# Sample attention of a streaming encoder step: appended new keys, hi/lo latent scores, one stacked rotary product, key scales spread by DMA

## The chip, the cores and the metric

The kernel runs on one core of a Trainium2 chip. The metric is the device time of one execution in microseconds (us), the median of three runs. Five engines work side by side, each with its own list of instructions, and wait for one another only through semaphores: TensorE (PE, matrix products; its weight loads are listed as PEld), VectorE (DVE), ScalarE (ACT), GpSimd (POOL) and SyncE (SP). PE reads SBUF and writes PSUM, which has eight banks of 512 fp32 columns. Every engine works through its own list strictly in the order in which it is written, so a wait at one place holds back all that stands behind it on that engine.

## The reference, cut to what matters

The program is one step of an encoder trunk: feed-forward blocks, a state-space mixer and one latent attention layer, for a prompt of 256 tokens and for 8 running streams of 16 new tokens each. The change touches the attention of the 8 streams ("sample attention"). Each stream has 512 past keys in a compressed cache and 16 new ones:

```python
def mla_expand(c_kv, w_kv_b, k_norm):          # c_kv: the latent, 256 wide
    kvb = (c_kv @ w_kv_b).reshape(b, S, MLA_HEADS, QK_NOPE + V_HEAD)   # 16 heads, 64 + 64
    k_nope = rmsnorm(kvb[..., :QK_NOPE], k_norm)
    return k_nope, kvb[..., QK_NOPE:]

def attend(q_nope, q_rope, k_nope, k_rope, v, q_pos, k_pos):
    s = (einsum('bqhd,bkhd->bhqk', q_nope, k_nope)
         + einsum('bqhr,bkr->bhqk', q_rope, k_rope)).astype(f32) * ATTN_SCALE
    s = where(mask, s, -inf)
    p = softmax(s, axis=-1).astype(v.dtype)
    return einsum('bhqk,bkhd->bqhd', p, v)
```

The kernel doesn't expand the past keys and values for the streams. It moves the key weights onto the query (a query in latent space, 256 wide), multiplies that with the cached latent, scales each score by the reciprocal norm of its key and head, adds the rotary score (32 wide), and takes the values from the cached latent too; the value weights are applied at the end.

## The kernel before, in words

Large fp32 products are made of three cheaper ones: an operand is split into a high part (ACT copies it into an fp32r tile, `hi_split`) and a low part (DVE subtracts, `lo_split`), and PE sums hi*hi, lo*hi and hi*lo. Smaller products are plain fp32 matmuls, which the profile lists as two passes each.

The attention layer has four stages. First the queries are made (loop over `cg`, 4 column groups by 3 token tiles); in it ACT and DVE also split the coming weight blocks, three blocks ahead, so the first three blocks of the output projection `wo` are split there too (L898 on, "QB + 2 * cg + b + 3"). Second, the prompt loop over 16 heads `x`: per head the prompt's attention and four `past_expand` steps, which only make the reciprocal norms of all past keys (`ksq`). Third, `QC`: 64 small products put the key weights `wkT` onto the sample queries, and ACT copies the results into `QC`. Fourth, the sample loop over 16 units `u`; a unit is one stream `b = u // 2` and 8 of its 16 heads (`g`), so that 8 heads by 16 queries fill 128 partitions. At its end 16 small products with the value weights (L2165, "the heads") and the output projection.

In the sample loop PE does, for a unit: the latent scores of the next unit (`s_nope`: past keys into bank 2, all 128 new keys of all streams into bank 5, L2112 and L2113), the turn of the previous unit's output (L2134), five transposes of the probabilities `Pb` (L2147), four transposes that spread the key scales over queries (`rq` to `rk`, L2121), the rotary scores (L2126, L2127), and the values (L2155, five accumulated products of 256 columns). DVE scales, adds and takes the maximum (L1595 to L1603), ACT takes the exponential (L1013, L1015) and copies (L1021, L1022, L1007), and DVE normalises the output (L1622). POOL copies the key scales (L592) and issues the loads of the next stream: `past_latent` (cacheT into `cTb`, cache into `cnat`, L561 and L566) and `past_rope` (L575). `cTb`, `cnat`, `Pb` and the rest have two buffers.

Of the kernel before, what the change touches and what calls it, by code (L numbers as in the profile page):

```python
# [31 lines left out]
P = 128  # L32
# [14 lines left out]
PAST = 512  # L47
MH, NOPE, ROPE, VH = 16, 64, 32, 64
# [38 lines left out]
def build(nc, T):  # L87

    ctx = ExitStack()
    with ctx:  # L90
# [21 lines left out]
        bank = [ctx.enter_context(nc.psum_tensor(f"bank{i}", [P, 512], F32)) for i in range(8)]  # L112
# [57 lines left out]
        with ExitStack() as mla:  # L170
# [13 lines left out]
            cTh = sb("cTh", [P, 2, 2, PAST], F32R, mla)  # L184
# [8 lines left out]
            with ExitStack() as split:  # L193
                cTb = sb("cTb", [P, 2, 2, PAST], F32, split)
            cTl = sb("cTl", [P, 2, 2, PAST], F32R, mla)
# [5 lines left out]
            gr = sb("gr", [P, ROPE], F32, mla)  # L201
            sm = sb("sm", [P, 128], F32, mla)
        Kp = lowA[:, :].rearrange("p (h t) -> p h t", h=MH)
        wkT = lowA[:, :].rearrange("p (h c) -> p h c", h=MH)
        QC = lowB[:, :].rearrange("p (k b h q) -> p k b h q", k=2, b=STREAMS, h=MH)
# [9 lines left out]
        def q_rope(e):  # L215
# [5 lines left out]
        ol = std[:, 0:KV_LORA]  # L221
        rbn = sqt[:, 0:2 * P].rearrange("p (g t) -> p g t", g=2)
        ksq = sqacc[:, :, :].rearrange("p a t -> p (a t)")[:, 0:STREAMS * 4 * MH].rearrange(
            "p (b s h) -> p b s h", b=STREAMS, s=4)
        krTb = ckv[:, 0:2, :].rearrange("p a c -> p (a c)")
        cqr = lowC[:, 0:TT * Q_LORA].rearrange("p (t c) -> p t c", t=TT)
        qgr = Pb[:, 0, 0:Q_LORA]
        mk = krTb[:, 0:TOK]
        praw = cTb[:, 0, :, 0:TOK]
        kvg = kn[:, 0, 0:KV_LORA + ROPE]  # L230
        rq = sq5
        rk = kn
# [94 lines left out]
        qc_ps = sem("qc_ps")  # L327
        qc_ev = sem("qc_ev")
        new_rq = sem("new_rq")
        new_rt = sem("new_rt")  # L330
        new_rk = sem("new_rk")
        rq_ready = sem("rq_ready")
        rt_done = sem("rt_done")
        rk_ready = sem("rk_ready")
# [36 lines left out]
        kr_ld = sem("kr_ld")  # L371
# [4 lines left out]
        s_out_ready = sem("s_out_ready")  # L376
        s_turn_ps = sem("s_turn_ps")
# [50 lines left out]
        acs_rows = nc.dram_tensor("acs_rows", (HEADS, TOK), F32, kind="Internal").ap()  # L428

# [25 lines left out]
        def _(pool):  # L455
# [74 lines left out]
            pool.dma_start(gr[:], T["gr"]).then_inc(w_ld, 16)  # L530
# [1780 lines left out]
```

## Time and profile before

| | us |
|---|---|
| median of three runs | 1978.94 (1974.6 to 1982.67) |
| the profiled execution | 1974.86 |
| its span in the profile | 1973.1 |
| sample loop, first score product to the first head product | 1487.5 to 1599.9 |

A line of the profile names a source line, an engine, an operation, the tiles and how often it came, then busy time and mean duration, then the idle time of the engine before it and who ended that. Matmuls are pipelined, so the time one costs is read from the distance between two starts, not from its duration. A matmul row marked x2 is one plain fp32 product in its two passes. "PEclk" is the share of the full 2.4 GHz clock that PE was granted.

### The profile page before, as it was taken

The page shows a single profiled execution, that of the slowest core. Times are in us where ns is not written, and L with a number is a line of the kernel's source. Part 1 is how long each engine was busy: PE and PEld are TensorE (multiplying, and loading weights), DVE is VectorE, ACT ScalarE, POOL GpSimd, SP SyncE. Part 2 cuts the span into 40 slices and gives each one's busy share as a digit, 9 for nine tenths or more (in the row PEclk, how much of TensorE's full clock was granted, in tenths as well). Part 3 has the DMA queues.
Part 4 walks back from the last instruction along what each step waited for, and adds up shares of the span by engine and source line. Part 5 has one row for each costly group of instructions (what it writes and reads, how often), then busy time and mean ns, then how long its engine had stood idle before and what let it go on. Part 6 is the DMA issues. An engine that isn't in the chain of part 4 may idle for free.

```text
span 1973.1 us, 28535 instructions
## 1 busy us (share of the span) xinstructions
PE 1901.7 (96%) x10641; PEld 1773.1 (90%) x10641; DVE 1136.4 (58%) x1800; ACT 819.5 (42%) x1428; POOL 235.3 (12%) x338
## 2 busy tenths in 40 slices
PE   9999998999998999999999999989999999999997
PEld 9999998788887999999999999876767779999997
DVE  6555448778779655445855544465654545555444
ACT  5333335555463433334533333355443324333233
POOL 1000110220210000011400002140012222000020
PEclk9999998999999999999999999899999999999999
DMA  5344444455342534444344444430022213444441
GB/s 198 126 128 128 139 148 141 135 176 203 111 181 91 174 125 126 130 136 129 115 140 128 128 135 132 166 101 22 33 66 79 80 51 119 125 124 126 136 138 64
DMA packets 63413, 243.33 MB, mean 123 GB/s; under 512 B 7681, under 2 KB 7761, under 8 KB 62049
## 3 DMA queue, kind: packets, MB, share of 16 engines
q1 hardware_dynamic: 54000, 196.67, 31.7%
q0 software_dynamic: 9328, 45.51, 6.6%
q8 instruction: 57, 0.93, 0.2%
q14 instruction: 28, 0.22, 0.0%
HBM read 230.32 MB, written 11.83 MB: 123 GB/s over the span
## 4 chain that ended last, share of the span: by engine, by line
PE 86%; DVE 7%; ACT 4%; issue 2%; POOL 0%; DMA 0%; SPq 0%; ACTq 0%; DVEq 0%; POOLq 0%
PE bank L1647 23%; PE bank L1649 23%; PE bank L1648 23%; PE bank L2155 2%; PE bank L2112 1%; PE bank L2057 1%; DVE wlo L1054 1%; PE bank L1844 1%; ACT seg L756 1%; PE bank L2059 1%; ACT kn L964 1%; PE bank L2058 1%; PE bank L1654 1%; PE bank L1655 1%; PE bank L1656 1%
## 5 line engine op out<-in xcount | busy, mean ns | idle before, releaser
L1647 PE MATMUL bank<-xh,whi 128*128 128x384 f32 x1960 | 665.7, 340 | 15.1 <-DVE xl L1064 13.2
L1649 PE MATMUL bank<-xh,wlo 128*128 128x384 f32 x1960 | 658.8, 336 | 0.0
L1648 PE MATMUL bank<-xl,whi 128*128 128x384 f32 x1960 | 658.8, 336 | 0.0
L1054 DVE TENSOR_TENSOR wlo<-raw,whi 128x1024 fp32r<-128x1024 f32 (+3 forms) x372 | 463.8, 1248 | 177.8 <-ACT whi L627 169.3
L627 ACT ACTIVATE whi<-raw 128x1024 fp32r<-128x1024 f32 (+2 forms) x369 | 378.9, 1029 | 296.4 <-PE bank L1649 282.4
L1647 PEld LDWEIGHTS bank<-xh,whi 128*128 128x128 f32 x1960 | 371.1, 189 | 25.3 <-issue 14.8
L1648 PEld LDWEIGHTS bank<-xl,whi 128*128 128x128 f32 x1960 | 371.2, 189 | 1.8 <-issue 1.2
L1649 PEld LDWEIGHTS bank<-xh,wlo 128*128 128x128 f32 x1960 | 370.5, 189 | 0.0
L1647 PE MATMUL bank<-ah,whi 128*128 128x384 f32 x704 | 237.2, 337 | 3.5 <-DVE tu L1075 3.3
L1074 DVE TENSOR_TENSOR tg<-bank,rstd 128x384 f32<-128x384 f32 x88 | 49.1, 557 | 331.1 <-PE bank L1649 330.5
L1649 PE MATMUL bank<-ah,wlo 128*128 128x384 f32 x704 | 236.8, 336 | 0.0
L1648 PE MATMUL bank<-al,whi 128*128 128x384 f32 x704 | 236.8, 336 | 0.0
L646 ACT ACTIVATE tg<-tg 128x384 f32<-128x384 f32 x88 | 46.4, 527 | 349.7 <-DVE tu L1075 349.7
L1647 PEld LDWEIGHTS bank<-ah,whi 128*128 128x128 f32 x704 | 132.6, 188 | 4.7 <-DVE tu L1075 4.7
L1648 PEld LDWEIGHTS bank<-al,whi 128*128 128x128 f32 x704 | 132.6, 188 | 0.0
L1649 PEld LDWEIGHTS bank<-ah,wlo 128*128 128x128 f32 x704 | 132.6, 188 | 0.0
L468 POOL TENSOR_TENSOR sqacc<-h 128x384 f32<-128x384 f32 x6 | 5.8, 975 | 804.9 <-DVE h L1102 759.6
L636 ACT ACTIVATE xh<-h,gains 128x384 fp32r<-128x384 f32 x64 | 37.0, 611 | 119.2 <-DVE h L1102 102.6
L470 POOL TENSOR_TENSOR sqt<-h 128x384 f32<-128x384 f32 x42 | 36.9, 878 | 288.6 <-DVE h L1102 266.4
L1545 DVE TENSOR_REDUCE sqacc<-kn 128x8 f32<-128x512 f32 x64 | 42.5, 683 | 49.8 <-ACT kn L964 49.7
L2057 PE MATMUL bank<-wkh,cTh 128*128 128x512 f32 x128 | 56.5, 441 | 5.1 <-ACT kn L964 4.5
L471 POOL TENSOR_TENSOR sqacc<-sqacc,sqt 128x384 f32<-128x384 f32 x42 | 58.0, 1381 | 3.3
(379 smaller groups left out, 2280.7 us busy)
## 6 DMA issues: line engine op xcount, KB each, us to landing
raw<-in_stream SPq DMA_DIRECT2D x372, 512.0 KB, 3.6
S<-in_ssm POOLq DMA_DIRECT2D x4, 2048.0 KB, 9.1
out_ssm_s<-S POOLq DMA_DIRECT2D x4, 2048.0 KB, 8.0
cTb<-in_cacheT POOLq DMA_DIRECT2D x16, 512.0 KB, 3.8
seg<-acs_rows POOLq DMA_DIRECT2D x12, 512.0 KB, 5.1
lowC<-in_cache POOLq DMA_DIRECT2D x8, 512.0 KB, 3.8
h<-in_x SPq DMA_DIRECT2D x2, 768.0 KB, 5.9
lowA<-in_wkT POOLq DMA_DIRECT2D x4, 384.0 KB, 5.5
```

What stands on the lines that cost most here:

```text
L471: step(pool.tensor_tensor(acc, acc, sqt[:, :], ALU.add))
L627: A(whi[:, r, 0:w], raw[:, r, 0:w], ACT.Copy).then_inc(hi_ready, 1)
L636: A(xh[:, k, :], h[:, k, :], ACT.Copy, scale=gains[:, m, k:k + 1]).then_inc(xh_ready, 1)
L646: A(tg[:, j, :], tg[:, j, :], ACT.Silu).then_inc(sg_ready, 1)
L1054: V.tensor_tensor(wlo[:, r, 0:w], raw[:, r, 0:w], whi[:, r, 0:w].bitcast(F32), ALU.subtract).then_inc(lo_ready, 1)
L1074: V.tensor_tensor(tg[:, j, :], bank[2 * j][:, 0:TOK], r, ALU.mult)
L1545: V.reduce_sum(ksq[:, b, st, 8 * g:8 * g + 8], kn[:, w % 2, 0:512].rearrange("p (h d) -> p h d", h=8), axis=AX.X).then_inc(past_sum, 1)
L1647: M(out, whi[:, r, ws], mh_(k), start=first and k == k0, stop=False)
L1648: M(out, whi[:, r, ws], ml_(k), start=False, stop=False)
L1649: ins = M(out, wlo[:, r, ws], mh_(k), start=False, stop=last and k == k1 - 1)
L2057: M(bank[w % 2][:, :], ch, wkh[:, k, half], start=k == 0, stop=False)
L2155: ins = M(bank[7][:, 256:512], PT[:, tiles(j)], cnat[:, b % 2, j, :] if j < 4 else ckv[:, 2, :], start=j == 0, stop=j == 4)
```

## The change

Only the sample attention and what prepares it are touched.

1. Each stream's 16 new keys are appended to its 512 past keys (`KEYS = 528`); the scores, the maximum and the exponential take all 528 in one instruction each. PSUM is declared as four pairs of banks, so that one DVE instruction reads 2 x 264 columns.
2. The latent scores become three-part products: the latent queries are split into `QCh` and `QCl` (in the tiles `whi` and `wlo`), the cached latent of each stream is split again into `cTh` and `cTl` (`keys_split`), from stream 2 on out of one single landing buffer `craw`.
3. The rotary score becomes one product with 96 stacked rows (hi, lo, hi of the query against hi, hi, lo of the key). For it `kraw` (one buffer) gets the rotary keys three times by DMA.
4. The key scales are turned once, written to memory (`rs_rows`), and read back for each unit by a DMA that repeats each row 16 times (`rs_spread`). The POOL copies and PE's turns for them are gone.
5. DVE normalises the probabilities (`Pb`), not the output; the values are made turned, once per stream and half of the latent (`s_values`), two units later. The turns of the output are gone.
6. The splits of the first three `wo` blocks move from the query stage to the end of the sample loop, since their tiles are in use. The loads of `wkT` are written behind the first two stores of `rs_rows` in POOL's list.
7. In the prompt loop: the rotary queries are stacked (x = 2, 4, 6), and the root and reciprocals of the scales of streams 0 to 5 are taken at x = 14.

```diff
@@ POOL @@
+            pool.wait_ge(rs_ev, 2)
+            pool.dma_start(rs_past(0, 6, 0, 3 * P), rsT[0:6 * MH, :]).then_inc(rs_st, 16)
+            pool.dma_start(rs_past(0, 6, 3 * P, P), rsT2[0:6 * MH, 0:P]).then_inc(rs_st, 16)
             for x in range(0, MH, MH // 4):
                 pool.wait_ge(qk_ps, x + MH // 4)
                 pool.dma_start(wkT[0:QD, x:x + MH // 4], T["wkT"][:, x:x + MH // 4]).then_inc(wkT_ld, 16)
...
+            def past_keys(b):
                 if b < 2:
...
+                    pool.wait_ge(qc_ps, 8)
+                    pool.wait_ge(past_lo, STREAMS + b)
+                    pool.dma_start(craw, T["cacheT"][b]).then_inc(c_ld[b % 2], 16)
+            def past_rope(b):
...
+                pool.dma_start(kraw[:, 0:PAST], T["krcT"][b]).then_inc(rope_ld, 16)
+                pool.dma_start(kraw[:, PAST:KEYS], kr_spread(b)).then_inc(rope_ld, 16)
+            def past_values(b):
+                pool.wait_ge(po_ps, MH + 2 * max(b - 1, 0))
                 pool.dma_start(cnat[:, b % 2], T["cache"][b]).then_inc(cn_ld[b % 2], 16)
+                pool.dma_start(vnew[0:STEPS, b % 2, :], ckv[STEPS * b:STEPS * b + STEPS, 2, :]).then_inc(cn_ld[b % 2], 16)
...
+            for u in range(2, UNITS):
+                b = u // 2 + 1
+                if u % 2 == 0 and b < STREAMS:
+                    past_keys(b)
+                    past_rope(b)
...
+                past_rstd_rows(u)
+                if u % 2 and b < STREAMS:
+                    past_values(b)
@@ ACT @@
+            def keys_split(b):
+                s = b % 2
+                act.wait_ge(c_ld[s], 16 * (STREAMS // 2 + b // 2 + 1))
...
+                A(cTh[:, s, :, 0:PAST], craw if b >= 2 else cTb[:, s, :, 0:PAST], ACT.Copy)
+                A(cTh[:, s, :, PAST:KEYS], cT[:, :, SEQ + STEPS * b:SEQ + STEPS * b + STEPS], ACT.Copy).then_inc(past_hi, 1)
+                act.wait_ge(rope_ld, 80 + 32 * (b + 1))
+                A(k_stack(b), kraw, ACT.Copy).then_inc(stack_hi, 1)
...
+            for u in range(UNITS):
                 if u >= 2:
+                    s_latent(u - 2)
                 if u + 1 < UNITS:
                     s_exp(u + 1)
+                s_turned(u)
+                if u % 2 == 0 and 2 <= u // 2 + 2 < STREAMS:
+                    keys_split(u // 2 + 2)
@@ DVE @@
+                step(V.tensor_tensor(p, pair[1][:, :, 0:KEYS // 2], r, ALU.mult))
+                V.tensor_tensor(p, p, pair[2][:, :, 0:KEYS // 2], ALU.add).then_inc(s_added, 1)
...
             for u in range(UNITS):
                 dve.wait_ge(s_exp_ready, u + 1)
+                step(V.reciprocal(sm[:, o + 5:o + 6], sm[:, o + 4:o + 5]))
+                V.tensor_scalar(Pb[:, s, 0:KEYS], Pb[:, s, 0:KEYS], sm[:, o + 5:o + 6], None, ALU.mult).then_inc(p_ready, 1)
                 if u + 1 < UNITS:
                     s_max(u + 1)
+                if u % 2 == 0 and 2 <= u // 2 + 2 < STREAMS:
+                    keys_split(u // 2 + 2)
@@ PE @@
+                    for k in range(2):
+                        M(out, qh, cTh[:, s, k, t], start=k == 0, stop=False)
+                        M(out, qh, cTl[:, s, k, t], start=False, stop=False)
+                        M(out, ql, cTh[:, s, k, t], start=False, stop=k == 1)
+                for a in range(2):
+                    ins = M(pair[2][:, a, 0:264], q_stack(b)[0:3 * ROPE, g, :], k_stack(b)[:, 264 * a:264 * a + 264],
+                            start=True, stop=True)
...
             for u in range(UNITS):
                 if u + 1 < UNITS:
+                    s_scores(u + 1)
+                if u >= 2:
+                    s_values(u - 2)
+                pe.wait_ge(p_ready, MH + u + 1)
+                pe.wait_ge(pt_ev, MH + u)
                 for j in range(5):
                     ins = nc.tensor.transpose(bank[6][:, tiles(j)] if j < 4 else bank[0][:, 0:P], Pb[:, u % 2, tiles(j)], ident[:, :])
```

What POOL does in the sample loop for one stream before: the latent of the next stream as soon as its scores are free (`sc_ps`), then the values (`lowC` is `cnat`), copies of the scales, then the rotary keys.

```order
L561 DMA cTb<-in_cacheT 128x1024 [waits sc_ps]
L566 DMA lowC<-in_cache 128x1024 [waits po_ps]
L592 COPY sq5<-sqacc 128x128 [waits rt_done]
L592 COPY sq5<-sqacc 128x128 x3
L575 DMA ckv<-in_krcT 32x512 [waits sc_ps]
```

And now, for the values of stream b and then the keys of stream b + 1 (`lowA` is `craw`, `sq5` is `kraw`, `kn` the spread key scales):

```order
L610 DMA lowC<-in_cache 128x1024 [waits po_ps]
L611 DMA ckv<-ckv 16x256
L598 DMA lowA<-in_cacheT 128x1024 [waits past_lo,qc_ps]
L605 DMA sq5<-in_krcT 96x512 [waits stack_lo]
L606 DMA sq5<-kr_rows 96x1x16
L616 DMA kn<-rs_rows 128x1x528 [waits s_added] x2
```

The load of the keys moved behind that of the values, whose wait (`po_ps`) asks for both value products of stream b - 2.

DVE in the sample loop before, one unit:

```order
L1615 TENSOR_TENSOR sm<-sm 128x1 [waits s_exp_ready]
L1616 RECIPROCAL sm<-sm 128x1 [waits dve_chain]
L1608 COPY lowB<-bank1 128x2x128 [waits s_turn_ps,dve_chain]
L1588 MEMSET Pb 128x128 [waits pt_ps]
L1595 TENSOR_TENSOR Pb<-bank2,kn 128x512 [waits sc_ps,rk_ready,dve_chain]
L1596 TENSOR_TENSOR Pb<-bank5,sqt 128x16
L1597 TENSOR_TENSOR Pb<-Pb,bank4 128x512 [waits dve_chain]
L1600 TENSOR_REDUCE sm<-Pb 128x1 [waits s_added]
L1603 TENSOR_SCALAR sm<-sm 128x1 [waits dve_chain]
L1622 TENSOR_SCALAR std<-bank7,sm 128x256 [waits po_ps]
```

And now, an even unit with the split of the keys two streams ahead (L1684 to L1690), and the head of the next unit:

```order
L1720 RECIPROCAL sm<-sm 128x1 [waits s_exp_ready]
L1721 TENSOR_SCALAR Pb<-Pb,sm 128x528 [waits dve_chain]
L1709 TENSOR_TENSOR Pb<-pair1,kn 128x528 [waits sc_ps,rk_ld1,pt_ps]
L1710 TENSOR_TENSOR Pb<-Pb,pair2 128x528 [waits dve_chain]
L1712 TENSOR_REDUCE sm<-Pb 128x1 [waits s_added]
L1713 TENSOR_SCALAR sm<-sm 128x1 [waits dve_chain]
L1684 TENSOR_TENSOR cTl<-lowA,cTh 128x2x512 [waits past_hi]
L1686 TENSOR_TENSOR cTl<-cT,cTh 128x2x16
L1690 TENSOR_TENSOR wkh<-sq5,wkh 32x528 [waits stack_hi]
L1720 RECIPROCAL sm<-sm 128x1 [waits s_exp_ready]
```

The split stands ahead of the next unit's normalisation, in one list with it.

POOL between the prompt loop and the sample loop, after (before, the four loads of `lowA`, which is `wkT`, stood right behind the six of `cTb` and waited for `qk_ps` alone):

```order
L574 DMA cTb<-in_cacheT 128x2x512 [waits past_ps] x4
L585 DMA rs_rows<-std 96x384 [waits rs_ev]
L586 DMA rs_rows<-sqt 96x128
L589 DMA lowA<-in_wkT 96x1024 [waits qk_ps] x4
L594 DMA cTb<-in_cacheT 128x2x512 [waits past_ps]
L605 DMA sq5<-in_krcT 96x512 [waits rope_ld]
```

`rs_ev` at this place is set by ACT's copies at the end of the prompt loop's last head.

## Rows read from the trace of the kernel before

**Rows 1.** The page: engines over the span, and the chain that ended last.
```profile
PE 1901.7 (96%) x10641; PEld 1773.1 (90%) x10641; DVE 1136.4 (58%) x1800; ACT 819.5 (42%) x1428; POOL 235.3 (12%) x338
PE 86%; DVE 7%; ACT 4%; issue 2%; POOL 0%; DMA 0%; SPq 0%; ACTq 0%; DVEq 0%; POOLq 0%
```
**Rows 2.** Stretch, busy of each engine, PEclk; and lines: durations ns, first and last start.
```profile
1487.50:1600.00 112.50, 107.28 (x530) 78.42 (x532) 62.35 (x207) 39.17 (x113) 25.85 (x83) 1.00 0.21 70
...
L2112 PE MATMUL bank<-cTb,lowB x64: 592/592/697, 1487.5 to 1587.2; 128*128 128x512 f32 x64
...
L2165 PE MATMUL bank<-lowB,wv x64: 272/273/325, 1599.9 to 1604.9; 128*64 128x128 f32 x64
```
**Rows 3.** Timeline of PE, one unit: start us, duration us, engine, line, operation.
```profile
1541.38 0.38 PE L2113 MATMUL bank<-cT,lowB 128*128 128x128 f32 x2
...
1542.36 0.60 PE L2121 MATMUL bank<-ident,sq 128*128 128x128 f32 x4
1542.80 1.02 PE L2126 MATMUL bank<-ckv,Qs 96*128 96x512 f32 x2
...
1543.88 1.89 PE L2155 MATMUL bank<-lowC,rstd 128*128 128x256 f32 x8
...
1546.04 1.02 PE L2112 MATMUL bank<-cTb,lowB 128*128 128x512 f32 x2
...
1547.98 0.39 PE L2113 MATMUL bank<-cT,lowB 128*128 128x128 f32 x2
```
**Rows 4.** Timeline of DVE, the same unit.
```profile
1544.18 0.69 DVE L1595 TENSOR_TENSOR Pb<-bank,kn 128x512 f32<-128x512 f32 x1 [1.53 <-PE bank L2127]
...
1545.79 0.69 DVE L1600 TENSOR_REDUCE sm<-Pb 128x1 f32<-128x512 f32 x1
...
1546.78 0.15 DVE L1603 TENSOR_SCALAR sm<-sm 128x1 f32<-128x1 f32 x1
```
**Rows 5.** Timeline of ACT, the same unit.
```profile
1546.96 0.72 ACT L1013 ACTIVATE Pb<-Pb,sm 128x512 f32<-128x512 f32 x1 [3.15 <-DVE sm L1603]
1547.59 0.19 ACT L1013 ACTIVATION_READ_ACCUMULATOR Pb<-Pb,sm 128x1 f32 x1
```
**Rows 6.** Timeline in the prompt loop: splits of one stream's latent, and a scaling.
```profile
1404.27 0.35 DVE L1570 TENSOR_SCALAR Pb<-Pb,sm 128x256 f32<-128x256 f32 x1
...
1406.22 1.07 ACT L956 ACTIVATE cTh<-cTb 128x1024 fp32r<-128x1024 f32 x1
...
1407.32 1.23 DVE L1540 TENSOR_TENSOR cTl<-cTb,cTh 128x1024 fp32r<-128x1024 f32 x1 [0.54 <-ACT cTh L956]
```
**Rows 7.** Line L1654: one of three equal groups of three-part products with 288 columns.
```profile
L1654 PE MATMUL bank<-whi,kxh x24: 289/295/299, 960.3 to 969.4; 128*128 128x288 f32 x24
```
**Rows 8.** DMA issues (KB each, median us to landing); two loads in flight, last column GB/s.
```profile
cTb<-in_cacheT POOLq DMA_DIRECT2D x16, 512.0 KB, 3.8
...
lowA<-in_wkT POOLq DMA_DIRECT2D x4, 384.0 KB, 5.5
...
1490.00:1491.00 1.00, 1.00 (x6) 0.59 (x5) 0.00 (x0) 0.59 (x1) 0.00 (x0) 1.00 1.02 410
```
**Rows 9.** Timeline of POOL: a load of the values, which waited for PE.
```profile
1546.51 0.53 POOL L566 DMA_DIRECT2D lowC<-in_cache  x1 [6.77 <-PE bank L2155]
```
**Rows 10.** Timeline around the end of the prompt loop: POOL, ACT and PE.
```profile
1461.13 0.51 POOL L554 DMA_DIRECT2D lowA<-in_wkT  x1 [15.48 <-PE bank L2046]
...
1476.59 1.28 ACT L993 ACT_TABLE_LOAD   x1
...
1477.45 9.01 PE L2095 MATMUL bank<-Qs,lowA 96*128 96x128 f32 x64 [1.78 <-DVE xl L1577]
```
**Rows 11.** Stretches of the query stage: PE, PEld, DVE, ACT, POOL busy, then PEclk.
```profile
1307.00:1310.00 3.00, 0.35 (x4) 0.09 (x1) 2.67 (x4) 2.85 (x7) 2.92 (x4) 1.00 0.14 14
1310.00:1313.00 3.00, 2.76 (x8) 1.54 (x9) 2.62 (x12) 1.75 (x6) 1.64 (x5) 0.74 0.83 274
```
**Rows 12.** Timeline of PE in the query stage: the wait for POOL's rows.
```profile
1310.24 0.64 PE L1979 MATMUL bank<-ident,kn 128*96 128x128 f32 x4 [2.89 <-POOL kn L544]
```

More of the change, by code:

```diff
@@ L111, in build @@
         rows = sb("rows", [P, 2, TT])
-        bank = [ctx.enter_context(nc.psum_tensor(f"bank{i}", [P, 512], F32)) for i in range(8)]
+        pair = [ctx.enter_context(nc.psum_tensor(f"pair{i}", [P, 2, 512], F32)) for i in range(4)]
+        bank = [pair[i // 2][:, i % 2, :] for i in range(8)]
         with ExitStack() as ffn:
@@ L327, in build @@
         qc_ps = sem("qc_ps")
+        qc_hi = sem("qc_hi")
         qc_ev = sem("qc_ev")
[L329 to L334, printed above, removed]
+        stack_hi = sem("stack_hi")
+        stack_lo = sem("stack_lo")
+        rs_turn_ps = sem("rs_turn_ps")
+        rs_ev = sem("rs_ev")
+        rs_st = sem("rs_st")
+        rk_ld = [sem(f"rk_ld{i}") for i in range(2)]
         s_added = sem("s_added")
@@ L1026, in _ @@
+            act.wait_ge(sc_ps, UNITS)
+            for b in range(AHEAD):
+                hi_split(WO + b)
+            for n in range(UNITS - 2, UNITS):
+                s_latent(n)
             for x in range(MH // 2):
@@ L1619, in _ @@
                 if u + 1 < UNITS:
                     s_max(u + 1)
[L1621 to L1623 removed]
+                if u % 2 == 0 and 2 <= u // 2 + 2 < STREAMS:
+                    keys_split(u // 2 + 2)
+            for b in range(AHEAD):
+                lo_split(WO + b)
             for x in range(MH // 2):
@@ new lines, in s_scores, with s_values @@
+                for a in range(2):
+                    ins = M(pair[2][:, a, 0:264], q_stack(b)[0:3 * ROPE, g, :], k_stack(b)[:, 264 * a:264 * a + 264],
+                            start=True, stop=True)
+                ins.then_inc(sc_ps, 1)
+            def s_values(n):
+                b, c = divmod(n, 2)
+                pe.wait_ge(pt_ev, MH + 2 * b + 2)
+                pe.wait_ge(cn_ld[b % 2], 32 * (b // 2 + 1))
+                if b:
+                    pe.wait_ge(s_out_kept, n - 1)
+                for j in range(5):
+                    v = cnat[:, b % 2, j, tiles(c)] if j < 4 else vnew[:, b % 2, tiles(c)]
+                    ins = M(bank[1 if c else 7][:, 0:256], v, PTs[:, b % 2, j, :], start=j == 0, stop=j == 4)
+                ins.then_inc(po_ps, 1)
@@ L2148, in _ @@
                 ins.then_inc(pt_ps, 1)
-                if u + 1 < UNITS:
-                    s_rope(u + 1)
-                pe.wait_ge(pt_ev, MH + u + 1)
-                if u % 2 == 0:
-                    pe.wait_ge(cn_ld[b % 2], 16 * (b // 2 + 1))
-                for j in range(5):
-                    ins = M(bank[7][:, 256:512], PT[:, tiles(j)], cnat[:, b % 2, j, :] if j < 4 else ckv[:, 2, :],
-                            start=j == 0, stop=j == 4)
-                ins.then_inc(po_ps, 1)
-            s_turn(UNITS - 1)
+            s_values(UNITS - 2)
+            s_values(UNITS - 1)
             pe.wait_ge(s_out_kept, 2 * STREAMS)
```

337 lines of the change are left out of this document (184 added, 153 removed).

## The prediction

> **What bounds the kernel now.** I read the page first: PE is busy 96% of the span and carries 86% of the chain that ended last [rows 1]. The changed stage is the sample loop, from the first score product at 1487.5 to the first head product at 1599.9: 112.4 us for 16 units, PE busy for 107.3 of them at full clock [rows 2]. The timeline of one unit shows why: the last score product of a unit starts at 1541.38 and that of the next at 1547.98, a period of 6.60 us without an idle entry on PE [rows 3]. DVE and ACT wait in each unit, DVE 1.53 for PE and ACT 3.15 for DVE [rows 4, 5]. So PE sets the pace there, and everybody else has slack.
>
> **What PE saves.** From start to start [rows 3]: a plain product of 128 columns costs 0.22, the four turns of the scales 0.44 (0.11 each), one of 512 columns 0.86 (1.08 for the rotary pair with its 128 new keys), the values 2.16 (10 passes), the latent scores 2.16. Three-part products of 288 columns: 72 of them from 960.3 to 969.4 [rows 7], 0.13 each; at 264 columns 0.12. A unit was 2.16 + 0.22 (output turn) + 0.54 (five turns) + 0.44 + 1.08 + 2.16 = 6.60. Now: 12 + 2 products of 0.12 = 1.67, five turns 0.54, values 2.16 (half of a stream's ten products of 256 columns) = 4.37. PE alone would give 16 x 2.23 = 36 us back. I don't think it gets them, because the loop stops being PE's.
>
> **The new cycle.** The latent of stream b (3 to 7) is split in ACT's and DVE's lists inside unit 2b - 4, ahead of the next exponential and the next normalisation. Its load stands in POOL's list behind the values' load of stream b - 1, and that waits for both value products of stream b - 3, which PE does in unit 2b - 3: later than the place where ACT and DVE already stand and wait. So once per stream the whole loop waits for a transfer that nothing hides. Queued behind the waiting split are, on ACT, `s_latent` and the exponential of unit 2b - 2, on DVE the normalisation of unit 2b - 3 and all after it; PE runs dry. I follow one turn, from T, the end of the add of unit 2b - 3 (on the PE side the clock starts 1.3 earlier, when ACT's copies let `s_values` begin):
> - PE: values 2.16, turns 0.54, scores 1.67, values 2.16 make 6.53, so `po_ps` at T + 5.2.
> - POOL: 0.3 to the issue (the 6.77 of idle in [rows 9] end some 0.3 after the product's modelled end, [rows 3]); two issues of 0.53 for the values and the 16 new rows come first. A 512 KB load lands 3.8 after its issue, and two together move 0.41 MB per us [rows 8]: 1.28 of moving, 2.5 fixed. The keys stand behind 0.54 MB: 2.5 + 1.06 / 0.41 = 5.1 after the first issue, T + 10.6. The rotary rows (0.2 MB) land at about T + 11.2.
> - ACT: split 1.07 and 0.2 for the new keys, to T + 11.9; rotary copy of 528 columns 0.74 (as the 0.72 of [rows 5]), to T + 12.7.
> - DVE: 1.23 [rows 6] + 0.17 + 0.7 (rotary low part) to T + 14.1; reciprocal 0.16 and scaling of 528 columns (0.35 for 256 [rows 6], so 0.48) to 14.75; multiply and add at 0.71 each (0.69 for 512 [rows 4]) with their handovers 1.46, to 16.2; maximum and scaling 0.9; ACT's exponential with its sum 0.83 and a handover [rows 5]; reciprocal and scaling 0.7; multiply and add 1.46: T + 20.15.
> Two units thus take 20.15 us against 13.2 now. Units with neither a split nor a load would take about 4.0 to 4.4.
>
> **The loop summed.** Up to the first T (unit 3), with the splits of streams 1 and 2 served in line on ACT and DVE: scores 1.7, multiply-add 1.46, maximum 0.9, exponential 0.88, ACT's split 2.0, DVE's rest 1.4; normalise and multiply-add 2.1; maximum, exponential, ACT's copies of the turns 0.8, split, rest 6.0; 2.1; and the last unit 3.9: 22.5. Then five turns, 100.8. After the last T, unit 14 waits for its spread scales, whose DMA stands in POOL's list behind that same values' load: 5.2 + 0.3 + 1.1 + 2.5 + 0.8 / 0.41, and 1.46, 11.4 (rounding up to the issue of the row's own DMA). Unit 15 4.0; its maximum, exponential, scaling 2.6; turns, copies, four half-streams of values and the last copy 7.2: 25.2. Together 148.5 against 112.4: **+36.1**. Bounds: a fixed part of 1.7 instead of 2.5 gives 6 x 0.9 = -6; 0.3 MB per us and slower starts give +7.
>
> **Before the loop.** The `wkT` loads were issued up to 1461.1, long before their product at 1477.45, which waited for DVE [rows 10]. Now they stand behind ACT's copies of the turned scales at about 1475.5 and two stores: first issue 1476.7. Alone they take 2.5 + 1.57 / 0.41 = 6.3; the 5.5 for a 384 KB load in company [rows 8] points to 7.3 or 8. At 7.3 the product starts at 1484.0. The cache load of stream 0 lands behind it, ACT's split of stream 0 stands ahead of its copies of `QC`, to 1487.4. DVE now subtracts each of the eight results too, and PE's fifth waits for DVE's first, at 1489.7, then four of 1.13, DVE's last, ACT's table load 1.28 [rows 10] and two copies: the scores begin near 1497 instead of 1487.5, **+9.5**. The additions inside the prompt loop (two subtractions of 1.23, a table load, three reciprocals, four turns) delay its end by some 1.6, but that lies inside this wait for the loads. Bounds: +6 (loads at 6.3 and a prompt loop unhurt) to +13.
>
> **The query stage.** In the fourth column group DVE and ACT no longer split two `wo` blocks; PE stood idle 2.89 for POOL's rows there, POOL's last steps took over a microsecond beside DVE's two subtractions, and DVE was busy 2.67 of 3 [rows 11, 12]. I take **-2.5** (2 x 1.23, bounds -2.9 and 0). The same three splits come back at the end of the loop: 3 x 1.07 on ACT and 3 x 1.23 on DVE beside 4.3 of value products, hidden, or +3 if the values' last copy waits for them.
>
> **The clock.** PE will stand idle some 9 us per stream. The rows show the price of one such hole: after a stretch with 0.35 of 3 us busy the next one has 0.74 of the clock, with PE busy [rows 11], that is some time at 1.2 GHz and then 2.4 again. In each turn this can hit the scores of the next unit (1.67 doubled, of which 0.85 is covered) and one value product: 0.8 a turn, **+4**, bounds 0 and +10.
>
> **The sum.** -2.5 + 9.5 + 36.1 + 4 = +47.1 on an execution of 1974.86, whose span is 1973.1: 2022. The median is 4.1 above that execution, so I forecast 2026.
>
> The Trainium skill, DMA: Bandwidth & Descriptors, "Anatomy of one DMA — SWDGE (gpsimd) path", gives 2.0 us plus the bytes at 436 GB/s for a DMA from GpSimd. For 512 KB that is 3.2 against the 3.8 of [rows 8], so the trace doesn't quite agree. By the page's figures the keys of a turn would land 0.7 earlier, six times: an estimate of 2022 in place of 2026.
>
> **Rivals.**
> - *The loads come in time* (POOL passes its wait before ACT gets there, say because PE is ahead). For it: POOL issues within 0.3 of its release [rows 9]. Against it: the lists above; PE can't do the values before the scores of unit 2b - 2. A turn would be maximum 0.9, exponential 0.9, two copies 1.2, split 2.0, rest 1.4, 2.1 and 3.95: 12.4. The loop then is 22.5 + 62 + 18.6 = 103.1, -9.3; with -2.5 + 9.5 and no clock loss -2: 1977, no change.
> - *The splits run beside the units and PE sets the pace*, 4.4 a unit: 71 and 12 at the ends, -29, in all -22: 1957. For it: DVE and ACT idle in every unit now. Against it: their lists are strict, and one unit's chain through DVE and ACT is already 4.0.
> - *PE stays slow.* If the clock didn't come back between the holes, every PE piece on the turn would double: 3.8 up to `po_ps`, 0.9 for the next scores, 2.7 for values and turns ahead of the next: 7.4 a turn, +37 in place of +4, 2059. For it: the holes are long. Against it: [rows 11] show it back within a few us. The Trainium skill, TensorE: Matmul & The Clock Gate, "HAM oscillation — how this bites in real kernels", describes this very pattern, short bursts between DMA waits running at half clock each time; no trace here has such a loop yet.
> - *The three-part products aren't cheap at 264 columns*: at 0.22 each, as a plain pass pair of 128 [rows 3], the scores would take 3.1, +1.4 twice a turn at most: 2040.
>
> **Chances.** The forecast 0.77, loads in time 0.11, PE's pace 0.04, slow clock 0.05, dear products 0.03. The range: the forecast's low bounds are -2.9 + 6 + 30 + 0 = +33, 2012, its high ones 0 + 13 + 43 + 10 = +66, 2045; I reach down to 2002 for landings shorter than any row shows. This kernel's measurement can tell 0.5%, some 10 us, from no change: faster than 1969 0.05 (PE's pace and a little of the first rival), within 0.09, slower 0.86.
>
> **What would show it.** After: POOL's issue of the craw load right behind a wait on the value products, with ACT's `cTh` copy waiting 5 to 6 us for that DMA, five times, 20 us apart; PE near 50% busy in the loop, PEclk below 1 in it; QC's first product waiting for the `wkT` DMA to about 1482 (its clock less 2.5); scores of a unit 1.7 on PE; the loop about 148 us. I am wrong if ACT's split never waits for a DMA from stream 3 on, or if units come at an even 4.4 to 6.

## The result: slower by 3.7%, 5 us beyond the range

The changed kernel takes 2050.12 us (median of 4 runs, 2044.24 to 2052.22) against 1976.77 (4 runs, 1968.76 to 1982.67): ratio 1.0369, 95% interval 1.0324 to 1.0414. The forecast was 2026 with a range up to 2045. The profiled execution took 2044.24, its span 2042.4: +69.3 on the span of before, where my terms (+47.1) made +47.

First the page, then the loop as one stretch (columns: from and to, length, busy us of PE, PEld, DVE, ACT, POOL with the number of instructions, granted clock as a share of 2.4 GHz, busy share of the DMA engines, GB/s), then the lines where the stages begin (durations ns, first and last start). They answer to [rows 1, 2].

```profile
PE 1889.3 (93%) x10584; PEld 1777.2 (87%) x10584; DVE 1144.4 (56%) x1733; ACT 827.3 (41%) x1427; POOL 245.0 (12%) x315
...
PE 81%; DVE 8%; ACT 5%; DMA 3%; issue 2%; POOL 1%; SPq 0%; ACTq 0%; DVEq 0%; POOLq 0%
```
```profile
1498.00:1670.00 172.00, 95.31 (x464) 83.30 (x462) 64.00 (x120) 43.46 (x104) 27.58 (x48) 0.73 0.28 71
```
```profile
L2083 PE MATMUL pair<-ident,kn x48: 270/272/288, 1290.5 to 1313.7; 128*96 128x128 f32 x48
...
L2149 PE MATMUL pair<-lowA,lowB x32: 272/273/377, 1333.7 to 1459.2; 96*128 96x128 f32 x32
...
L2230 PE MATMUL pair<-cTh,whi x64: 283/406/589, 1497.7 to 1656.7; 128*128 128x264 f32 x64
...
L2268 PE MATMUL pair<-lowB,wv x64: 272/273/323, 1670.2 to 1675.2; 128*64 128x128 f32 x64
```

PE is busy 95 us of a loop of 172, at 0.73 of its clock; before it was 107 of 112 at full clock. Stage by stage (us; "prompt" is the first prompt score, L2045 before and L2149 after):

| stage | before | after | change | forecast |
|---|---|---|---|---|
| first turned query to prompt | 47.1 | 43.2 | -3.9 | -2.5 |
| prompt to QC's first product | 139.8 | 151.5 | +11.7 | } +9.5 |
| QC's first product to scores | 10.1 | 12.5 | +2.4 | } |
| scores to heads (the loop) | 112.4 | 172.5 | +60.1 | +36.1, clock +4 |
| heads to the end | 373.2 | 372.2 | -1.0 | 0 |

A turn of the loop is two units with the load of one stream; "PE's turns" are its transposes of `Pb`, something else. One turn of the loop, first POOL, then ACT, DVE and PE (start us, duration us; in brackets the idle time before and what ended it). T, the end of unit 5's add, is 1544.54. PE's idle time between its value products and its next turns, 11.21 here, is called the hole.

```profile
1550.27 0.57 POOL L610 DMA_DIRECT2D lowC<-in_cache  x1 [19.50 <-PE pair L2246]
...
1551.34 0.56 POOL L598 DMA_DIRECT2D lowA<-in_cacheT  x1
...
1553.10 1.22 POOL L616 DMA_DIRECT2D kn<-rs_rows  x2
```
```profile
1557.13 1.06 ACT L1058 ACTIVATE cTh<-lowA 128x1024 fp32r<-128x1024 f32 x1 [9.81 <-DMA lowA<-in_cacheT]
```
```profile
1558.34 1.23 DVE L1684 TENSOR_TENSOR cTl<-lowA,cTh 128x1024 fp32r<-128x1024 f32 x1 [12.87 <-ACT cTh L1059]
...
1561.77 0.70 DVE L1710 TENSOR_TENSOR Pb<-Pb,pair 128x528 f32<-128x528 f32 x1
...
1566.12 0.71 DVE L1709 TENSOR_TENSOR Pb<-pair,kn 128x528 f32<-128x528 f32 x1 [1.12 <-PE pair L2234]
```
```profile
1561.18 1.33 PE L2258 MATMUL pair<-ident,Pb 128*128 128x128 f32 x5 [11.21 <-DVE Pb L1721]
```

This is the forecast's turn: POOL, which waited 6.77 in [rows 9], waits 19.50 and issues right behind the value products, ACT's split waits for the keys, DVE for ACT, PE for DVE. ACT waits 9.81 for the keys, where I had 5 to 6. The keys are there at T + 12.6 (12.6 to 13.9 in the five turns, 13.2 in the mean) where I had T + 10.6, and the next add ends at 1567.56, T + 23.0 instead of T + 20.95 (20.15 and 0.8 for the clock). From the values' issue at 1526.72 to the one at 1645.54 there are five turns, 23.76 each. The clock and the transfers in the hole:

```profile
1545.00:1549.00 4.00, 4.00 (x29) 3.75 (x28) 0.44 (x2) 1.75 (x5) 0.00 (x0) 1.00 0.00 0
1549.00:1553.00 4.00, 0.97 (x5) 0.51 (x3) 0.00 (x0) 0.00 (x0) 2.73 (x5) 1.00 0.35 110
1553.00:1557.00 4.00, 0.00 (x0) 0.00 (x0) 0.00 (x0) 0.00 (x0) 1.32 (x3) 0.61 0.95 247
...
1561.00:1565.00 4.00, 3.80 (x16) 3.40 (x17) 2.96 (x7) 1.48 (x4) 0.00 (x0) 0.50 0.01 4
```
```profile
lowA<-in_cacheT POOLq DMA_DIRECT2D x6, 512.0 KB, 6.1
```

While the keys travel (1551.34 to 1557.13), the DMA engines move some 250 GB/s (in the window from 1553 on they are 0.95 busy at 247), where the window of [rows 8] that I had sized them by moved 410 at 1.02; a load of keys takes 6.1 from issue to landing (the median), not 3.8. And the scores behind the hole run at 0.50, 1.2 GHz.

Ahead of the loop, QC's first product, which waited 1.78 for DVE in [rows 10], waits for its loads (PE's timeline):

```profile
1485.15 9.67 PE L2210 MATMUL pair<-Qs,lowA 96*128 96x128 f32 x64 [8.93 <-DMA lowA<-in_wkT]
```

### The profile page after: what moved, and what is told of

Read it like the earlier page. It is cut to its first block, busy times and chain, and to the rows that moved or that the text cites. A ratio compares the mean times of both kernels' runs of the same rounds, so it can differ in the third digit from the quotient of the medians.

```text
span 2042.4 us, 28316 instructions
## 1 busy us (share of the span) xinstructions
PE 1889.3 (93%) x10584; PEld 1777.2 (87%) x10584; DVE 1144.4 (56%) x1733; ACT 827.3 (41%) x1427; POOL 245.0 (12%) x315
## 3 DMA queue, kind: packets, MB, share of 16 engines
q1 hardware_dynamic: 54000, 196.67, 30.7%
## 4 chain that ended last, share of the span: by engine, by line
PE 81%; DVE 8%; ACT 5%; DMA 3%; issue 2%; POOL 1%; SPq 0%; ACTq 0%; DVEq 0%; POOLq 0%
PE pair L1751 22%; PE pair L1752 22%; PE pair L1753 22%; PE pair L2246 2%; DMA lowA<-in_cacheT 2%; PE pair L2167 1%; DVE wlo L1141 1%; PE pair L1758 1%; PE pair L1760 1%; PE pair L1759 1%; PE pair L1948 1%; ACT seg L801 1%; ACT kn L1010 1%; PE pair L1967 1%; PE pair L2169 1%
## 5 line engine op out<-in xcount | busy, mean ns | idle before, releaser
L1751 PE MATMUL pair<-xh,whi 128*128 128x384 f32 x1960 | 664.2, 339 | 15.2 <-DVE xl L1151 13.3
L1753 PE MATMUL pair<-xh,wlo 128*128 128x384 f32 x1960 | 657.7, 336 | 0.0
L1752 PE MATMUL pair<-xl,whi 128*128 128x384 f32 x1960 | 657.5, 335 | 0.0
L1751 PEld LDWEIGHTS pair<-xh,whi 128*128 128x128 f32 x1960 | 370.5, 189 | 25.7 <-issue 14.9
L1752 PEld LDWEIGHTS pair<-xl,whi 128*128 128x128 f32 x1960 | 370.4, 189 | 1.8 <-issue 1.2
L1753 PEld LDWEIGHTS pair<-xh,wlo 128*128 128x128 f32 x1960 | 369.9, 189 | 0.0
L1751 PE MATMUL pair<-ah,whi 128*128 128x384 f32 x704 | 237.0, 337 | 3.5 <-DVE tu L1162 3.3
L1752 PE MATMUL pair<-al,whi 128*128 128x384 f32 x704 | 236.5, 336 | 0.0
L1753 PE MATMUL pair<-ah,wlo 128*128 128x384 f32 x704 | 236.5, 336 | 0.0
L1752 PEld LDWEIGHTS pair<-al,whi 128*128 128x128 f32 x704 | 132.4, 188 | 0.0
```

Source lines behind the costliest of these rows:

```text
L1751: M(out, whi[:, r, ws], mh_(k), start=first and k == k0, stop=False)
L1752: M(out, whi[:, r, ws], ml_(k), start=False, stop=False)
L1753: ins = M(out, wlo[:, r, ws], mh_(k), start=False, stop=last and k == k1 - 1)
```

## The experiments

Each edit is to the changed kernel, if nothing else is said; the diffs are shortened. Each ratio is to the kernel before, run beside it, with its 95% interval. The medians of the kernel before lay between 1974.2 and 1981.6 in these sets, so a few us between two experiments are read from the traces, not from the medians. The turn is the mean over five, from one issue of a stream's values (in same_wait over four, keys' issues) to the next; the loop is first score to first head. Single turns scatter: in the changed kernel and in wkt_first, whose loops have the same lists, ACT's split starts 6.1 to 7.9 after the values' issue, and a turn takes 21.3 to 24.1.

**keys_first** and **rows_first**: which of the two loads behind the values' wait makes the turn? In keys_first the keys go ahead:

```diff
+            past_keys(2); past_rope(2)          # ahead of the loop over u
                 past_rstd_rows(u)
-                if u % 2 == 0: past_keys(b); past_rope(b)   # was ahead of the rows
+                if u % 2: past_keys(b + 1); past_rope(b + 1)
                 if u % 2: past_values(b)
```

> POOL issues the keys and rotary rows of stream b+1 ahead of the values of stream b; nothing else differs. Theory (the cycle over POOL's list): the turn of two units falls from 23.5 us to some 12.4 to 13.5, ACT's split copy waits for no DMA from stream 3 on, the sample loop goes from 172.5 to about 120 (the tail, where the scale rows of unit 14 stand behind a values load, stays near 30), the kernel from 2050 to about 1997. Rival (the splits in line and the slow clock are the cost, the load only fills their shadow): the turn stays above 18 us, the kernel above 2020.

2030.23 us, ratio 1.0253 (1.0221 to 1.0285); turn 20.25, loop 155.1. My theory missed by 33 us, and the rival's numbers came out for another reason. ACT's split waits for no DMA from stream 3 on; DVE waits instead, for the scale rows of unit 2b, which still stand behind the same values' load:

```profile
1557.93 0.71 DVE L1711 TENSOR_TENSOR Pb<-pair,kn 128x528 f32<-128x528 f32 x1 [6.62 <-DMA kn<-rs_rows]
```

rows_first is the other half (`past_rstd_rows(u + 1)` ahead of `past_values(b)` for odd u, the keys behind the values).

> POOL issues the scale rows of unit 2b ahead of the values of stream b; the keys stay behind them. It is the counterpart of keys_first (keys ahead, rows behind: a turn of 20.2 us). Theory (two cycles over one wait, each enough by itself; the keys' is the longer by the splits behind it): a turn of 21.5 to 22.6 us as without the rows (22.5), a tail from the last values' issue to the heads of 13 us instead of 24.7, the loop 155, the kernel 2032 to 2036. Rival (the scale rows make the longer cycle, the keys hardly one of their own): a turn below 18 us, the kernel below 2010.

2041.45 us, ratio 1.031 (1.0268 to 1.0351), 5 us above the range expected; turn 22.72, at the upper end of what was expected, loop 163.2 instead of 155. The tail was 19.3, not 13: unit 15's rows still stood behind the last values, and DVE waited 4.4 for them. So there are two cycles over one wait, 22.7 by the keys and 20.3 by the rows, and freeing either leaves the other.

**values_late**: both at once, by moving what they stand behind.

```diff
-                if u % 2 and b < STREAMS:
-                    past_values(b)
+                if u % 2 and u > 3:
+                    past_values(b - 1)
```

> Only POOL's load of a stream's values moves, to behind the scale rows of unit 2b+1 (two positions later); keys, rotary rows and scale rows keep their order among themselves, wkT stays where the change put it. Theory (one load with a late wait holds up two others, the keys of the next stream and the scale rows of unit 2b; each alone keeps the turn above 20 us): moving it frees both, the turn is 11.8 to 12.5 us as with all three edits, the loop 104 to 108, the kernel 1980 to 1986 (all_three's 1974 and the 7 us of wkT). Rival (the keys must also go first): a turn of 15 us or more, above 1998.

1982.06 us, ratio 1.0017 (0.9997 to 1.0038). Turn 12.1, loop 103.7: from a loss of 3.7% to none by moving one load in POOL's list. Keys and rows keep their order; it was the wait in front of them. POOL waits 4.7 to 5.3 there instead of some 20, and ACT's split no longer waits:

```profile
1549.82 0.58 POOL L610 DMA_DIRECT2D lowC<-in_cache  x1 [4.90 <-PE pair L2246]
...
1558.70 1.06 ACT L1058 ACTIVATE cTh<-lowA 128x1024 fp32r<-128x1024 f32 x1
```

**split_late**: ACT's and DVE's `keys_split(u // 2 + 2)` behind odd u instead of even.

> ACT's and DVE's splits of a stream's keys move one unit later in their lists (behind unit 2b-3 instead of 2b-4); POOL's order is that of the change. Theory (the cycle is load, split, scores, value products, and the place of the split only decides who else stands behind it): keys at T + 12.6, split and its rest 3.4, scores 1.7, values up to the release 2.5, so a turn of 20 us still, the kernel near 2030. Rival (the place of the split is what costs, the wait hides behind the unit's other work): the turn falls to 12 to 15 us, below 2005.

2056.3 us, ratio 1.0397 (1.0363 to 1.0431), 26 us above what I expected; turn 24.0. ACT no longer waits for the keys, but the turn is no shorter, for DVE stands at the scale rows:

```profile
1569.93 0.71 DVE L1709 TENSOR_TENSOR Pb<-pair,kn 128x528 f32<-128x528 f32 x1 [12.51 <-DMA kn<-rs_rows]
```

Moving the split gains nothing. My explanation of the 20 us that I expected (the keys' own path) isn't what the trace shows either: the rows took over before it.

**same_wait** and **no_rows**: why do keys land 2 us later than forecast? same_wait issues keys and rotary rows first behind the same wait, and the values last. no_rows leaves the scale rows of units 4 to 15 out.

```diff
-                if u % 2 == 0 and b < STREAMS:
+                if u == 2:
                     past_keys(b)
                     past_rope(b)
...
                 if u % 2 and b < STREAMS:
+                    pool.wait_ge(po_ps, MH + 2 * (b - 1))
+                    if b + 1 < STREAMS:
+                        past_keys(b + 1); past_rope(b + 1)
                     past_values(b)
```

> POOL waits for the value products as after the change, but then issues keys and rotary rows of stream b+1 first and the values behind them; scale rows of unit 2b stay behind all of it. Theory (the wait is what holds the keys; the 528 KB in front cost two issues of 0.54 us and 1 to 2 us of landing): the keys land 4.1 us after their issue instead of 6.1, the turn falls from 23.8 to 20.7 us, the kernel from 2050 to about 2035. Rival (the landing is slowed by the small rows behind the keys, not by the values in front): the turn loses only the 1.1 us of issues, 2045.

2040.51 us, ratio 1.032 (1.0283 to 1.0357). The keys land in 4.1, as expected, and the turn is 21.3 (expected 20.7): the wait alone costs most of what a turn is above the 12.1 of values_late, the 528 KB in front 2.5 (two issues of 0.5 and the later landing).

> The spread loads of the scale rows of units 4 to 15 are left out (these units take the scales of units 2 and 3). Theory (the 264 KB rows issued right behind the keys share the DMA engines with them): craw lands 4.1 us after its issue instead of 6.1, the turn falls from 23.5 to 21.5 us, the wait of 10.3 us for the rows in unit 14 goes (4 us of tail), 2050 becomes about 2036. Rival (the keys' landing is slowed by the values' load ahead of them and the rotary rows behind): the turn stays within 0.5 us of 23.5, only the tail's 4 us go, 2046.

2035.4 us, ratio 1.0284 (1.026 to 1.0309). The keys land in 5.2 to 5.3, the turn is 22.54. So the rows behind the keys cost 1.2 a turn where I expected 2 (0.9 of it is the landing), and the tail gave 12 instead of 4 (12.7 from the last values' issue to the heads, against 24.7). The kernel's 2036 came out by luck: the two misses cancel. After the change DVE waits there for unit 14's rows:

```profile
1653.01 0.71 DVE L1709 TENSOR_TENSOR Pb<-pair,kn 128x528 f32<-128x528 f32 x1 [10.35 <-DMA kn<-rs_rows]
```

**warm_pe, warm_pe20, warm_pe27**: what the slow clock costs. 40, 20 and 27 products that nothing reads fill PE's hole.

```diff
                     s_values(u - 2)
+                if u in (3, 5, 7, 9, 11):
+                    pe.wait_ge(pt_ev, MH + u)
+                    for _ in range(40):             # 20, 27
+                        M(bank[0][:, 256:512], ident[:, :], wv[:, 0, 0:256], start=True, stop=True)
                 pe.wait_ge(p_ready, MH + u + 1)
```

> 40 products of 128x256 with the unit matrix (0.216 us each at full clock, 8.6 us) fill PE's hole of 11.3 us in units 3, 5, 7, 9 and 11; nothing reads their results. Theory (the hole takes the clock away, and turns and scores behind it run at 1.2 GHz): with PE busy in the hole the turns of a unit take 0.6 instead of 1.3 us and its scores 1.7 instead of 3.4, and the turn loses the 1.1 us that DVE's multiply waits for the scores, up to 2.4: the kernel goes from 2050 to 2038 to 2045. Rival (what follows the hole is hidden behind DVE and ACT): no change within 3 us. If the products themselves run at 1.2 GHz they take 17 us and the kernel is slower, 2075.

2062.58 us, ratio 1.0426 (1.0389 to 1.0464): turn 26.1. The fill was twice as long as meant: a product of 128x256 in plain f32 is two passes, as the timeline of the value products says, where four products are listed x8. It outlasted the hole, so the run says nothing of the clock's price.

> As the run before it, with 20 instead of 40 products: a product of 128x256 is two passes of 0.217 us (80 records took 17.4 us there), so 20 take 8.7 us, inside the hole of 11.3. Theory (the hole takes the clock away; DVE's multiply waits 1.1 us a turn for scores at 1.2 GHz, and PE's turns ahead of them cost 0.7 more): the turn falls from 23.8 to 22.0 to 22.7 us, the kernel from 2050 to 2040 to 2045. Rival (what PE does behind the hole is not on the turn's path): 23.8 stays, 2050.

2049.13 us, ratio 1.0356 (1.0322 to 1.0391); turn 22.9, and the five differ. PE still stood idle ahead of its turns, and then once more, 0 to 1.0, ahead of the scores:

| | 1 | 2 | 3 | 4 | 5 |
|---|---|---|---|---|---|
| idle ahead of PE's turns | 4.0 | 4.2 | 2.6 | 2.9 | 2.0 |
| clock of the scores behind | 0.50 | 0.50 | 1.00 | 0.50 | 1.00 |
| turn of the loop | 24.2 | 24.2 | 21.9 | 22.7 | 21.6 |
| ACT's split to the next T | 11.2 | 10.4 | 9.2 | 10.2 | 9.6 |

The fourth turn in three stretches, then two stretches of the third:

```profile
1609.00:1615.00 6.00, 5.27 (x25) 4.30 (x23) 0.66 (x1) 1.39 (x3) 0.99 (x2) 1.00 0.89 207
1615.00:1618.00 3.00, 0.77 (x5) 0.53 (x5) 2.87 (x7) 0.70 (x2) 0.00 (x0) 1.00 0.08 23
1618.00:1621.00 3.00, 2.47 (x11) 2.47 (x12) 1.99 (x5) 1.48 (x4) 0.00 (x0) 0.50 0.00 0
```
```profile
1592.00:1595.00 3.00, 0.42 (x2) 0.01 (x1) 2.72 (x6) 1.06 (x4) 0.00 (x0) 1.00 0.27 55
1595.00:1598.00 3.00, 2.39 (x18) 2.15 (x19) 2.14 (x4) 0.72 (x2) 0.00 (x0) 1.00 0.00 0
```

So within one run the scores came at either clock, and at full clock the way from split to next T was 0.6 to 2.0 shorter. The turns also differ in when their keys landed (6.2 to 8.5 after the values' issue), which is no matter of the clock.

> 27 products instead of 20 or 40: 27 x 2 x 0.217 = 11.7 us, the whole of PE's hole of 11.3 us, so that PE doesn't stand idle ahead of the turns and scores. With 20 it still stood 2.9 to 4.2 us and the scores behind ran at a clock of 0.50. Theory (any rest of a hole takes the clock; at full clock the scores end 1.1 to 1.6 us earlier on the turn's path): PE at 1.00 through the turn, a turn of 22.2 to 22.8 us against 23.8, the kernel 2042 to 2045. Rival (the clock costs nothing on the turn's path, DVE and ACT cover the scores): 23.8 stays, 2050.

2043.94 us, ratio 1.0338 (1.03 to 1.0377); turn 22.1. PE kept 1.00 through the hole and the scores:

```profile
1564.00:1568.00 4.00, 4.00 (x20) 3.44 (x19) 2.14 (x4) 2.09 (x4) 0.00 (x0) 1.00 0.38 70
1568.00:1572.00 4.00, 3.08 (x21) 2.32 (x19) 2.93 (x8) 1.11 (x3) 0.00 (x0) 1.00 0.00 0
```

The turn is 23.76 - 22.12 = 1.6 shorter. The keys landed 0.2 earlier in the mean, by chance, so 1.4 is the clock's, 7 us in five turns. Most of it, 1.15, lies between ACT's split and the next T, which is 10.42 to 10.46 in each turn of the changed kernel and 9.21 to 9.24 in four of the five here (9.59 in one). The kernel's time alone wouldn't show it: the two ratios' intervals (1.0324 to 1.0414, 1.0300 to 1.0377) overlap. The theory written ahead of this run, that any rest of a hole takes the clock, is refuted by turns 3 and 5 of warm_pe20.

**wkt_first**: the four `wkT` loads ahead of the wait for the turned scales and their stores.

> The four wkT loads are issued ahead of the wait for the turned scales and their two stores, as before the change; nothing else differs. Theory: the first QC product no longer waits 8.9 us for that DMA and starts 8 us earlier, the kernel goes from 2050 to about 2042. Rival (the wait only moves on): the split of stream 0, the scale rows or the eight copies with their subtractions end last anyway, the scores begin at most 3 us earlier, 2047 to 2050.

2039.49 us, ratio 1.0307 (1.028 to 1.0333). From prompt to QC's first product 144.2 instead of 151.5, to the scores 157.1 instead of 164.0: 7 us, with the wait gone (1.78 for DVE, as before the change). The loop is 168.9 instead of 172.5, its turn 23.1: four of 23.2 to 23.8 and one of 21.3, in which the keys came 1.1 earlier than in the mean and the clock was back sooner. Nothing in the edit touches the loop's lists, so I put those 3.6 us down to scatter, which isn't shown.

**all_three**: keys_first with the values' load moved as in values_late, and wkt_first.

> Keys and rotary rows ahead of the values, the values' load of stream b behind the scale rows of unit 2b+1, and the wkT loads issued first. Theory: the turn is 12.4 to 13.5 us, the tail 19 to 22, the loop 105 to 112, the wait for wkT is gone: 1968 to 1977, within 0.5% of the kernel before the change. Rival (in-line splits and the slow clock keep the loop long): 2000 to 2010.

1974.36 us, ratio 0.9977 (0.9955 to 0.9999), as expected; loop 104.4, 8 shorter than before the change, and scores 7.6 later (157.4 against 149.8 from prompt).

**spread_subs**: values_late and wkt_first, and DVE's two subtractions of the stacked query in two heads.

```diff
-                    if x == 6 and i in (1, 3):
+                    if x in (6, 8) and i == 1:
```

> values_late and wkt_first together, and DVE's two subtractions of the stacked query (1.22 us each), both inside head 6 of the prompt loop, are put one each into heads 6 and 8, at the place where odd heads have their split. Theory (two in one head stand on the loop's path, one hides as the splits do at 0.35): the prompt loop is 2 to 2.3 us shorter, its start to the first score product 155 instead of 157.4, the kernel 1972, 0.3% below before. Rival (the loop's 4.6 us come from elsewhere, copies on ACT or the new loads): 157.4 stays, 1974.

1974.3 us, ratio 0.9972 (0.9952 to 0.9992). The prompt loop gave somewhat more than expected (prompt to QC 141.4 instead of 144.3), the kernel less (1972 expected): QC to the scores took 14.8 instead of 13.1. ACT's split of stream 0 stands ahead of its copies of QC and waits 2.5 for its keys, which POOL issues behind its wait for the scales; PE's fifth product, now earlier, waits for DVE behind that:

```profile
1489.81 5.46 PE L2210 MATMUL pair<-Qs,lowA 96*128 96x128 f32 x32 [2.67 <-DVE wlo L1698]
```

**before_wo_late**: one part of the change alone, on the kernel before.

```diff
-                    hi_split(QB + 2 * cg + b + 3)      # and lo_split on DVE
+                    if QB + 2 * cg + b + 3 < WO:
+                        hi_split(QB + 2 * cg + b + 3)
...
+            for b in range(AHEAD):                     # behind the sample loop
+                hi_split(WO + b)
```

> The kernel before, with one part of the change alone: ACT and DVE split the first three wo blocks behind the sample loop instead of inside the fourth column group of the query stage. Theory: from the first turned query to the first prompt score 43.2 us as in every run after the change, instead of 47.1; at the loop's end the splits stand ahead of the heads and cost up to 3 us there; the kernel 1975 to 1979 against 1979. Rival (the 3.9 us come from something else of the change): 47.1 stays, the kernel 1979 to 1982.

1979.94 us, ratio 0.9998 (0.998 to 1.0015). First turned query to prompt 43.3 as expected, so the 3.9 us are this part's. They come back at the other end: loop 114.9 instead of 112.4, and the heads from first to last product take 8.1 instead of 5.0. After the change the heads take 5.0 (L2268 above); there the splits stand beside the last value products.

**early_keys0**: spread_subs, with `past_keys(0)` ahead of POOL's wait for the turned scales, and ACT's table load behind its two copies.

> The best version so far (values late, wkT first, subtractions spread) with two more moves: POOL issues the keys of stream 0 ahead of its wait for the turned scales, and ACT loads the exponential's table behind its two copies of the last scales instead of ahead of them. Theory: ACT's split of stream 0 no longer waits 2.5 us for its DMA, with PE's wait of 2.7 us for DVE behind it, and the table's 1.28 us leave the path to the first score: 3 to 4 us, the kernel 1970 to 1971, 0.45% below before. Rival (eight copies with two subtractions each set that stage's end anyway): 1.3 us, 1973.

1966.74 us, ratio 0.9936 (0.9914 to 0.9959): faster than both kernels, and more than expected. Prompt to QC 141.5, QC to the scores 9.3 (14.8 in spread_subs), loop 102.7. Its two moves weren't tried apart, so which of them gave the 5.5 is open. Its loop as one stretch:

```profile
1485.00:1587.00 102.00, 80.66 (x464) 70.38 (x464) 63.62 (x120) 43.69 (x104) 27.99 (x48) 0.93 0.41 118
```

PE has 80.7 us of work there against 107.3 before [rows 2], 27 less, and the loop is 9.7 shorter. It stands idle for 21 us instead of 5: each turn of 12 now runs through DVE and ACT, with the splits in line.

## Why the prediction was wrong in size and right in kind

- **The mechanism held.** PE stops being the bound, the split of stream b waits for a load that stands behind the value products of stream b - 3, five turns. keys_first, rows_first and values_late show that it is this wait; the rival in which loads come in time fell, and values_late is the kernel that it described (turn 12.4 forecast, 12.1 measured; loop 103.1 and 103.7).
- **The step that failed: "The keys stand behind 0.54 MB: 2.5 + 1.06 / 0.41 = 5.1 after the first issue, T + 10.6".** It was 6.9 in the turn shown and 7.3 in the mean of the five, and T + 13.2 for ACT (the first issue itself came 0.4 later than I had it). I took the rate of two large loads side by side; in the turn the engines were nearly as busy and moved 0.25 MB per us. In same_wait, without the 528 KB in front, the keys' own load takes 2.0 less, in no_rows, without the scale rows behind, 0.9 less; the two overlap and don't add up. I hadn't put the scale rows on the keys' path at all. The 2.6 a turn are 13 us in five turns, of the 20 by which the loop was off. My high bound of 0.3 MB per us gave +7 for the whole loop; even that end was too kind.
- **The clock**, forecast at 0.8 a turn, costs 1.4 (warm_pe27). It added next to nothing to the miss, by luck: from the keys to the next add I had 9.55 and 0.8 for the clock, 10.35, and it took 10.44, but at full clock it takes 9.2, so my chain through ACT and DVE was 0.3 too long. The rival in which the clock stays low fell: it is back at 1.00 before the next hole, each time. The Trainium skill, TensorE: Matmul & The Clock Gate, "HAM oscillation — how this bites in real kernels", has short bursts between DMA waits at half clock each time; this loop now agrees with it for the first burst after each hole, not for those behind.
- **Fill and tail.** Fill (first score to the first T) 23.7 against 22.5. Tail (last T to the heads) 30.7 against 25.2: the add of unit 14 ended at T + 14.9, not T + 11.4, its rows being late for the same reason as the keys. But 1.1 of those 3.5 is a slip in my sum: the terms that I wrote down (5.2, 0.3, 1.1, 2.5, 0.8 / 0.41 and 1.46) make 12.5, and I went on with 11.4. Together 1.2 + 5 x 2.7 + 5.5 = 20, which closes the loop. (The low bound has a slip too: 6 x 0.9 should be 6 x 0.8.)
- **ACT's wait** for the keys was 9.8 to 10.6, not 5 to 6: half of the miss is the late keys, the other half is that ACT stood at its split by about T + 3, not T + 5. That half moved nothing, since the wait ends with the keys.
- **Before the loop** +14.1 against +9.5. The loads stood late as I said (8.93 waited). The 4.6 too little is the prompt loop: "delay its end by some 1.6, but that lies inside this wait for the loads". It was 4.6 (the 11.7 of the table less the 7.15 by which the wait grew, 1.78 to 8.93), and it couldn't lie inside, because the loads are themselves issued behind ACT's copies at the loop's end; the whole delay comes on top. 2.9 of the 4.6 are the two subtractions in one head (spread_subs).
- **The query stage** -3.9 against -2.5: I counted DVE's two splits and left out that PE, idle less, keeps its clock (0.74 and 0.69 before from 1310 to 1316, 1.00 after; the 24 expansions behind are 11.0 us of work instead of 12.7).
- **One load alone.** The Trainium skill, DMA: Bandwidth & Descriptors, "Anatomy of one DMA — SWDGE (gpsimd) path", has 2.0 us plus the bytes at 436 GB/s, which would give 3.2 for the keys (an estimate); the trace has 6.1 in company and 4.1 in same_wait, and 3.5 for the values' load, the first of its batch. The measurements decide here.
- **Three-part products** at 264 columns cost 0.12 each at full clock, as forecast (from start to start, the third turn of warm_pe20).

I had one cycle in the chain of the loop and treated the scale rows only in the tail. That they were a second cycle of nearly the same length (20.3 against 22.7) changed no number of the forecast, but it would have misled the repair, as keys_first did. Open: what share of the low rate in the turn comes from the small rows (64 B pieces of the rotary rows, 1 KB rows of the values) and what from the number of transfers; it wasn't tried.

## What to carry to other kernels

On an in-order DMA-issuing engine, the latest wait in front of a load is that load's wait: go through the list once per transfer and ask what every transfer behind it needs, since freeing one may only hand the same wait to the next. Size a landing by the rate the engines moved in company like that of the new place, not by the cleanest window of the trace. A delay lies hidden inside a wait only if what ends the wait isn't itself behind the delay.

## What the hardware showed that I had not expected

- Filling most of the hole brought the clock back only in some turns. In warm_pe20 PE was busy for 8.6 us of the hole and then idle: behind 2.9, 4.0 and 4.2 us of idle time the scores ran at 0.50, just as after the whole hole, behind 2.0 and 2.6 at 1.00 (2.4 GHz). With the products up to PE's turns (warm_pe27) they ran at 1.00 in all five.
- DMA engines 0.95 busy moved 247 GB/s in one place and, at 1.02, 410 in another.
- The place of one load in one queue decided 69 us of loop: values_late moves the same bytes as the changed kernel, and its loop is 103.7 instead of 172.5.
